# A fourth seven-product step in the second part's first down half, for the last chunk of a hybrid decoder block

## The reference, cut to what matters

```python
def swiglu(h, wg, wu, wd):
    return (jax.nn.silu(h @ wg) * (h @ wu)) @ wd

x = x + 0.5 * swiglu(rmsnorm(x, ffn1_norm[i]), ffn1_wg[i], ffn1_wu[i], ffn1_wd[i])
x = x + hybrid_mixer(rmsnorm(x, mix_norm[i]), ...)
x = x + 0.5 * swiglu(rmsnorm(x, ffn2_norm[i]), ffn2_wg[i], ffn2_wu[i], ffn2_wd[i])
return rmsnorm(x, final_norm)
```

## Time and profile before

| | |
|---|---|
| runs | 1815.12 us median of 3 (1814.51 to 1815.33) |
| profiled execution, first to last instruction (its own time is not given apart from it) | 1810.6 us |
| PE busy | 1799.3 us, 8134 matmuls |
| DVE busy | 1555.0 us |
| ACT busy | 1022.7 us |
| seven-product steps in the program | 82 |

### The profile page before, as it was taken

The page is one execution under the profiler, slowest core; times in us unless marked ns, Lnnn a source line. Parts: engine busy times, 40 slices in busy tenths (PEclk is TensorE's granted clock), DMA queues, the critical chain, the costliest instruction groups (busy, mean ns, idle before and its releaser), DMA issues.

```text
span 1810.6 us, 21958 instructions
## 1 busy us (share of the span) xinstructions
PE 1799.3 (99%) x8134; PEld 1481.8 (82%) x8134; DVE 1555.0 (86%) x1863; ACT 1022.7 (56%) x1334; POOL 246.2 (14%) x442
## 2 busy tenths in 40 slices
PE   9999999999999999999999999999999999999998
PEld 7788888888888888888788888888888888888886
DVE  7999998889999977678667867899999889999987
ACT  6655555445555556556567745555555455555554
POOL 1111111001111100000123300111111000222100
PEclk9999999999999999999999999999999999999999
DMA  7676766667676766766443655667676666677764
GB/s 244 209 213 221 217 210 211 207 202 220 206 216 203 218 201 207 209 214 194 149 138 107 209 174 185 209 207 218 209 216 212 214 207 194 209 219 221 242 202 151
DMA packets 199289, 367.28 MB, mean 203 GB/s; under 512 B 19013, under 2 KB 23857, under 8 KB 199057
## 3 DMA queue, kind: packets, MB, share of 16 engines
q1 hardware_dynamic: 185008, 352.37, 62.5%
q0 software_dynamic: 11648, 12.02, 2.2%
q10 hardware_dynamic: 2528, 1.52, 0.3%
HBM read 350.11 MB, written 4.19 MB: 196 GB/s over the span
## 4 chain that ended last, share of the span: by engine, by line
PE 93%; DVE 5%; ACT 1%; DMA 1%; issue 0%; ACTq 0%; DVEq 0%
PE ps L771 23%; PE ps L773 23%; PE ps L772 23%; PE ps L789 7%; PE ps L791 7%; PE ps L790 7%; PE ps L838 2%; DVE w_lo L1820 2%; DVE wt_lo L1892 1%; DVE wt L1882 0%; ACT w_hi L1305 0%; PE ps L1069 0%; PE ps L1096 0%; DMA raw<-in_ffn_wu_dram 0%; PE ps L1071 0%
## 5 line engine op out<-in xcount | busy, mean ns | idle before, releaser
L1820 DVE TENSOR_TENSOR w_lo<-raw,w_hi 128x1024 fp32r<-128x1024 f32 x573 | 692.1, 1225 | 111.8 <-ACT w_hi L1305 107.8
L1305 ACT ACTIVATE w_hi<-raw 128x1024 fp32r<-128x1024 f32 x573 | 599.6, 1056 | 287.3 <-PE ps L773 197.8
L771 PE MATMUL ps<-w_hi,hT_hi 128*128 128x512 f32 x1308 | 512.4, 392 | 1.3 <-ACT gu L1399 1.2
L773 PE MATMUL ps<-w_hi,hT_lo 128*128 128x512 f32 x1308 | 509.6, 390 | 0.0
L772 PE MATMUL ps<-w_lo,hT_hi 128*128 128x512 f32 x1308 | 509.3, 389 | 0.0
L712 POOL DMA_DIRECT2D gu_raw<-gu_sq x352 | 187.5, 541 | 1077.2 <-DVE gu_sq L2066 1003.7
L1356 ACT ACTIVATE wt_hi<-wt 128x1024 fp32r<-128x1024 f32 x164 | 172.9, 1054 | 274.7 <-DVE wt L1882 274.7
L771 PEld LDWEIGHTS ps<-w_hi,hT_hi 128*128 128x128 f32 x1308 | 245.7, 188 | 52.0 <-ACT gu L1399 2.1
L773 PEld LDWEIGHTS ps<-w_hi,hT_lo 128*128 128x128 f32 x1308 | 245.6, 188 | 52.0
L772 PEld LDWEIGHTS ps<-w_lo,hT_hi 128*128 128x128 f32 x1308 | 245.7, 188 | 49.7
L1892 DVE TENSOR_TENSOR wt_lo<-wt,wt_hi 128x1024 fp32r<-128x1024 f32 x164 | 199.6, 1217 | 0.0
(11 more groups left out here) (312 smaller groups left out, 2219.6 us busy)
## 6 DMA issues: line engine op xcount, KB each, us to landing
raw<-in_ffn_wu_dram SPq DMA_DIRECT2D x176, 512.0 KB, 4.5
raw<-in_ffn_wd_dram SPq DMA_DIRECT2D x176, 512.0 KB, 4.8
raw<-in_ffn_wg_dram SPq DMA_DIRECT2D x175, 512.0 KB, 4.1
raw<-in_w_in_dram SPq DMA_DIRECT2D x88, 512.0 KB, 3.6
raw<-in_w_out_dram SPq DMA_DIRECT2D x32, 512.0 KB, 4.2
gu_raw<-gu_sq POOLq DMA_DIRECT2D x352, 32.0 KB, 3.5
x_parked<-x SPq DMA_DIRECT2D x8, 256.0 KB, 5.3
raw<-in_cmp_k_w_dram SPq DMA_DIRECT2D x8, 256.0 KB, 3.2
```

What stands on the lines that cost most here:

```text
L771: mm(o, x_hi, w_hi[:, s, kk, :], start=begin, stop=False, skip_group_check=skip)
L773: ins = mm(o, x_lo, w_hi[:, s, kk, :], start=False, stop=last and kk == GK - 1, skip_group_check=skip)
L1305: act.activation(w_hi[:, c % SLOTS, :, :], raw[:, c % SLOTS, :, :], ACT.Copy).then_inc(hi_ready, 1)
L1820: tt(w_lo[:, s, :, :], raw[:, s, :, :], w_hi[:, s, :, :].bitcast(F32), ALU.subtract).then_inc(lo_ready, 1)
```

## The change

The last chunk (number 10) gets a quad in the fourth place, which the second part had free. In the first half of down part 1 the slots L9 and R9 become a step P9, directly behind P5: L0 L2 L4 L6 L7 P1 R0 R2 R4 P3 L8 R6 P5 P9 R7 R8. The quad is made at g = 11 (DVE sums), 12 (ACT) and 13 (DVE low part, with a semaphore of its own, `last_gs_lo`, that PE waits for before P9). As the last paired slot is now 17 and not 15, the five residual steps of this half come two slots later (g = 20 to 24), with them the residual of block 1 (22 to 24), the x transposes (22 to 23) and the squares and gains at 23 and 25 (25 and 27). The second half's table is unchanged. Both FFNs use the table.

```diff
-QUADS = [4, 3]
+QUADS = [4, 4]
...
         [[(LEFT, 0), (LEFT, 2), (LEFT, 4), (LEFT, 6), (LEFT, 7), (PAIR, 1), (PAIR2, 1), (RIGHT, 0),
-          (RIGHT, 2), (RIGHT, 4), (PAIR, 3), (PAIR2, 3), (LEFT, 8), (LEFT, 9), (PAIR, 5), (PAIR2, 5),
-          (RIGHT, 6), (RIGHT, 7), (RIGHT, 8), (RIGHT, 9)],
+          (RIGHT, 2), (RIGHT, 4), (PAIR, 3), (PAIR2, 3), (LEFT, 8), (RIGHT, 6), (PAIR, 5), (PAIR2, 5),
+          (PAIR, 9), (PAIR2, 9), (RIGHT, 7), (RIGHT, 8)],
...
+def quad_place(n):
+
+    part = int(n >= PART0[1])
+    if n == NFC - 1:
+        return QUADS[1] - 1
     q = n - PART0[part]
-    return f * sum(QUADS) + part * QUADS[0] + q if q < QUADS[part] else None
+    return q if q < QUADS[part] - part else None
...
-X0_AT = 22
+X0_AT = 23
 TURN_STEPS = [0, 1, 2, 3, 14]
+LAST_SUMS = 11
...
+                        if kind == PAIR and part and q == 2 * PARTN[1] - 1:
+                            pe.wait_ge(last_gs_lo, f + 1)
...
+                        if part and g == LAST_SUMS + 1:
+                            gs_high(n_last, quad_no(f, n_last))
...
-                    tt(low, buf, high.bitcast(F32), ALU.subtract).then_inc(gu_lo, 1)
+                    tt(low, buf, high.bitcast(F32), ALU.subtract).then_inc(
+                        last_gs_lo if n == NFC - 1 else gu_lo, 1)
...
+                        if part and g == LAST_SUMS:
+                            gu_sums(f, n_last, quad_no(f, n_last))
+                        if part and g == LAST_SUMS + 2:
+                            gs_low(n_last, quad_no(f, n_last))
...
-                            if g == HALF[1] + 2:
+                            if g == HALF[1] + 4:
                                 residual(1, FFN0[f] + down_slot(1, 1), 1, half)
```

More of the change, by code:

```diff
@@ L151, in quad_no @@
     part = int(n >= PART0[1])
+    q = quad_place(n)
+    return None if q is None else f * sum(QUADS) + part * QUADS[0] + q
+def quad_place(n):
+    part = int(n >= PART0[1])
+    if n == NFC - 1:
+        return QUADS[1] - 1
     q = n - PART0[part]
-    return f * sum(QUADS) + part * QUADS[0] + q if q < QUADS[part] else None
+    return q if q < QUADS[part] - part else None
 R_FFN1B, R_CONV, R_ATT, R_FFN2B = range(4)
@@ L516, in build_program @@
         gs_hi_ready = sem("gs_hi_ready")
+        last_gs_lo = sem("last_gs_lo")
         prod_d = sem("prod_d")
@@ L985, in down @@
                         if kind == PAIR:
-                            seven_products(f, c + g, guT_hi, guT_lo, GK * q, gs_hi[:, q // 2, :, :],
-                                           gs_lo[:, q // 2, :, :], job_no(f, ("down", part, h)), p == at_[h][0],
+                            place = quad_place(PART0[part] + q // 2)
+                            seven_products(f, c + g, guT_hi, guT_lo, GK * q, gs_hi[:, place, :, :],
+                                           gs_lo[:, place, :, :], job_no(f, ("down", part, h)), p == at_[h][0],
                                            p == at_[h][-1])
@@ L1418, in gs_high @@
             def gs_high(n, quad, i=None):
-                q = n - PART0[int(n >= PART0[1])]
+                q = quad_place(n)
                 if quad is not None:
@@ L1488, in down @@
                         if part == 1:
-                            for n, g1 in enumerate((23, 25, 39)):
+                            for n, g1 in enumerate((25, 27, 39)):
                                 if g == g1 and (f or n < 2):
@@ L2171, in down @@
                                 x_operand(1, 0)
-                            if f == 1 and g in (23, 25, 39):
-                                final_gains((23, 25, 39).index(g))
+                            if f == 1 and g in (25, 27, 39):
+                                final_gains((25, 27, 39).index(g))
                 for n in range(1, PARTN[0]):
```

## The result

| | before | after |
|---|---|---|
| median of the runs, us | 1815.12 (5 runs, 1812.43 to 1815.38) | **1821.36** (5 runs, 1818.45 to 1822.44) |
| ratio to before, 95% interval | | 1.0037, 1.0027 to 1.0048 |
| profiled span, us | 1810.6 | 1816.6 |
| matmuls | 8134 | 8128 |
| second down part, first FFN, us | 107.13 | 109.39 (+2.26) |

The change costs 6.2 us between the two medians, and the ratio is 1.0037. The median lies in the range of the forecast, 1.8 us above its middle. One execution of the changed kernel, in e1_again, fell into a slow state (2592.09 us at a mean granted clock of 0.654) and is in no median and no ratio here. A "down part" in the table runs from the start of its first matmul to the start of the first matmul with the next stage's weights in the trace (in the second FFN to the end of the last).

What follows compares the result with a forecast made beforehand. PE, busy 99% of the span, was taken as the bound, so matmuls removed and waits added count in full: -1.36 + 5.82 = +4.46 us on 1815.12 gives 1819.6 us, range 1817.4 to 1822.8.

Steps and rivals of the forecast that it cites:

- The three matmuls fewer: In each FFN two ordinary slots of 12 matmuls become one step of 21: -0.68 us each, -1.36 us for both.
- P9 directly behind P5: PE waits at P9's first matmul with sums, which wait for P5's end: +2.91 us each FFN, +5.82 us both.
- S: Start of P5's last matmul on PE, 640.33 in the trace before; the forecast counts P9's times from it.
- P9's second half and slot 18, hidden: Low parts of P9's second sums and slot 18 reach PE in time, 0.4 and 0.6 us to spare: no cost.
- The quad, nothing: The quad's DVE and ACT work comes ahead of P5's sums: no cost, 0.5 us to spare in the first FFN.
- SP's loads: Slot 20's load waits for P9's T4, later loads behind it; rounded by S + 8.5, needed S + 13.3: hidden.
- the five residual steps: Moved two slots later; step 0 done at S + 10.9 against PE's need at S + 13.3: hidden, no cost.
- The clock stays at 1.00: PE's granted clock holds across P9's wait, idle about 2.6 us; rival that it falls: 3.1 us more, 1822.7 us, 6%.
- The stall is shorter: Rival: PE restarts sooner at P9 or recovers part of the wait, 1.5 to 2.4 us each: 1816.8 to 1818.6, 12%.
- no stall: Rival: P9's low parts release PE by S + 1.59, so only the three matmuls count: 1813.8 us, 3%.
- the median lies 4.5 us above the span: For the kernel before, the median of the runs was read as 4.5 us above the profiled span of 1810.6 us.

Runs made afterwards that it cites:

- e1_again: The changed kernel run again with no edit: 1821.33 us against 1814.39 for the kernel before, ratio 1.0041.
- e11_spread_half: Changed kernel with P3, P5, P9 apart (slots 9/10, 12/13, 16/17) and T1 and T3 sums released nine matmuls earlier: 1813.34 us, ratio 0.9999 to before.
- e4_adj: Against the changed kernel: P5 directly behind P3 (slots 12 to 15), P9 two ordinary slots again, quad unused: 1820.64 us, ratio 1.0035 to before.
- e7_half: Changed kernel with the sums for T1 and T3 released by the fourth product, nine matmuls before the step's end: 1816.07 us, ratio 1.0011 to before.
- e5_quad_only: Table of the kernel before with the change's other work; quad made but unused, residual steps at their old slots: 1814.56 us, ratio 1.0003 to before.
- e3_spread: Changed kernel with the steps apart, one ordinary slot between P3 and P5, two between P5 and P9: 1813.56 us, ratio 0.9997 to before.
- e8_longer: Changed kernel with one more DVE difference, read by nobody, ahead of P9's first low part: 1825.05 us, ratio 1.0054 to before.
- e9_spread_again: Second run, unedited, of the changed kernel with one ordinary slot between P3 and P5, two between P5 and P9: 1814.01 us, ratio 0.9999 to before.

## Why the prediction was right in its sign and short in its size

*The three matmuls fewer, -0.68 us for each FFN.* Right: e11_spread_half has them without the wait, at -0.62 and -0.64; e4_adj has the wait without them, at +2.98.

*P9 directly behind P5, +2.91 us.* Right, and to the last piece. The sums started 0.53 us behind S (0.53 forecast), the low part 2.59 later (2.59), PE 1.28 after that (1.27), and the matmul behind the wait was followed after 0.34 us (0.34). Wait and restart together are 2.81 + 0.11 us, and the part without a fall of the clock is +2.26 us where -0.68 + 2.91 = +2.23 was forecast. Each piece came from a row of the same instruction in another place of the trace. e4_adj shows that two steps side by side are enough for it, and e7_half that the release of the buffer starts it.

*P9's second half and slot 18, hidden.* Right: no wait of PE shows there. The lows of the slots 18 to 20 started at 646.27, 6.00 us behind S; 0.53 + 5.47 = 6.00 was the working.

*The quad, nothing, with P5's sums at about 632.8.* Right: they started at 632.31, 4.8 us ahead of PE's request, and e5_quad_only measures the cost at 0.00 us in both parts. SP's loads and the five residual steps, costed at nothing, show no wait of PE in after, and in e11_spread_half no cost above 0.06 us. ACT took up slot 20 at 647.36 in after and was done 1.06 us later, at S + 8.15, where S + 8.5 was worked out.

*The clock stays at 1.00.* **This is the step that failed.** The forecast let it stay at 1.00 over a standstill of 2.6 us, because the longest wait in the trace before, 1.17 us, had left it there, and gave the fall 6%. No row of before spoke for a wait twice as long, and the prediction said so; it should then have been near even odds, not one in seventeen. The runs show a fall in one of two places in three profiles with this wait, and a mean clock of 0.997 or 0.998 in all ten runs of the changed kernel (in e4_adj in two of five). With the wait cut, filled or shortened to 1.36 us, the four profiles show none. The price was nearly right: 1.33 us for a fall in after and 1.42 between the two parts of e4_adj, where 1.6 was worked out. With one fall the sum is 4.46 + 1.33 = 5.8 us, with two 7.1, and the measured 6.2 and, in e1_again, 6.9 lie between. The Trainium skill (TensorE: Matmul & The Clock Gate, HAM oscillation) lets the clock fall only behind idle gaps longer than this one; here a standstill of 2.65 us was enough, in some executions and not in others, and the measurement decides.

*The stall is shorter*, and *no stall*: the first did not happen, since three profiles gave 3.03 or 3.04 us between starts in both FFNs. The second named its own condition, that the sums do not wait for P5's end. e7_half made it true for T1 and T3 and brought two thirds of the loss back; e3_spread made it true by distance and landed within 0.2% of before.

One reading of the forecast is wrong without consequence: that the median lies 4.5 us above the span. In after a run's time lies 1.8 us above its own span (1818.45 against 1816.6), and 1.8 to 1.9 us in every later run, so the profile of before is of one of its fastest executions, near the lowest run of 1812.43. The sum does not use it.

Open is what decides in a single execution whether the clock falls. In after and e1_again it was the second FFN, in e4_adj the first. The wait was the same length in each. What is shown is only that it goes with PE's standstill.

## What to carry to other kernels

When two pieces of work share one buffer, putting them side by side puts its whole refill (release, making, hand-over) on the path of the engine that reads it; sum that chain from rows where each link already shows, and weigh it against what the extra piece saves, here 4.4 - 1.6 us against 0.7. Release a buffer by the reader that reads it last, part by part: moving one signal nine matmuls earlier was worth two thirds of the loss. And where a change makes PE stand longer than it does anywhere in the trace before, give the fall of the clock a price and a real chance: here 1.17 us was the longest wait that said anything, and 2.65 us was enough.

## What the runs showed of the hardware that was not expected

- A standstill of PE of 2.65 us was followed by about 3.4 us at half the clock in one of the two FFNs in each of three profiles (after, e1_again, e4_adj), and not in the other; at 3.78 us it was in both (e8_longer): in the second the clock fell within the wait and stayed low for 14 starts, in the first it fell only after PE had restarted (starts 0.34 and 0.27 us apart, then 0.43). Waits of 1.5 and 0.9 us close together, and waits of 1.36 us, left it at 1.00 in every profile.
- Matmuls with a weight of 32 columns of zeros, 11 in 2.71 us, left the clock at 1.00 through the place of the standstill and did not delay the product behind them: it started 1.27 us after DVE's low part had started, as without them.
- Loads that landed later moved a step's sums by 1.5 us between two executions of one kernel (e3_spread and e9_spread_again), enough to turn a gain of 0.3 us into a loss of 0.8 in one part.
